# Pooling chunks of the even layer moved, in pieces, into its attention; half of its output projection too; four heads at once in its softmax steps

## The reference, cut to what matters

```
z = rms_norm(x) @ w_in               # 1280 columns: u 512 | q 512 | k 128 | v 128
# pooling: 4 groups of 128 channels, trailing windows 2, 4, 8, 16
diff_g = window_sum(u_g) / count - u_g
ya_g   = (diff_g @ w_pool_g) * scale
# attention: 8 query heads, 2 key heads, chunks of 64; a chunk reads itself and the 2 before it
p  = exp(s - m) / (sum exp(s - m) + exp(sink - m)),  m = max(max s, sink)
yb = p @ v
x  = x + concat(ya, yb) @ w_out
x  = x + ffn(rms_norm(x))
```

## Time and profile before

| | |
|---|---|
| median of 3 runs | 1284.98 us (1284.3 to 1286.83) |
| profiled execution | 1286.24 us, its span 1284.1 us |
| PE busy | 1229.3 us, 96% |
| DVE busy | 814.2 us, 63% |
| POOL busy | 700.0 us, 55% |
| ACT busy | 262.0 us, 20% |
| mean granted TensorE clock | 0.986 |

### The profile page before, as it was taken

The page is one execution under the profiler, slowest core; times in us unless marked ns, Lnnn a source line. Parts: engine busy times, 40 slices in busy tenths (PEclk is TensorE's granted clock), DMA queues, the critical chain, the costliest instruction groups (busy, mean ns, idle before and its releaser), DMA issues.

```text
span 1284.1 us, 24797 instructions
## 1 busy us (share of the span) xinstructions
PE 1229.3 (96%) x9677; PEld 1193.1 (93%) x9677; DVE 814.2 (63%) x1174; ACT 262.0 (20%) x514; POOL 700.0 (55%) x565
## 2 busy tenths in 40 slices
PE   6978999999999999999999998999999999999995
PEld 6966799999999999999999985799999999999995
DVE  6988477777777732116544688666877887872221
ACT  3015332111111110002111165422112112110002
POOL 6732257556656666665644432156665665566661
PEclk9989999999999999999999999899999999999998
DMA  6311123222223232233222310132222222323221
GB/s 211 116 58 34 36 67 99 82 92 87 82 84 95 82 99 87 94 98 110 83 84 65 102 60 23 34 109 89 93 82 86 93 82 82 95 84 96 88 79 71
DMA packets 35524, 108.91 MB, mean 85 GB/s; under 512 B 5984, under 2 KB 7792, under 8 KB 35472
## 3 DMA queue, kind: packets, MB, share of 16 engines
q1 hardware_dynamic: 29232, 102.51, 24.7%
q10 hardware_dynamic: 6240, 5.64, 1.5%
HBM read 103.00 MB, written 5.13 MB: 84 GB/s over the span
## 4 chain that ended last, share of the span: by engine, by line
PE 88%; DVE 8%; ACT 2%; issue 1%; DMA 0%; POOL 0%; ACTq 0%; POOLq 0%; SPq 0%; DVEq 0%
PE psum L423 28%; PE psum L425 27%; PE psum L424 27%; DVE even_winsum L1340 1%; PE psum L741 1%; PE psum L608 1%; DVE small L1561 1%; DVE even_rope_swapped L1322 1%; PE psum L756 1%; DVE even_diff L1343 0%; DVE gate_tmp L1490 0%; PE psum L582 0%; PE psum L556 0%; DVE diff_probs L1576 0%; DMA x<-in_x 0%
## 5 line engine op out<-in xcount | busy, mean ns | idle before, releaser
L423 PE MATMUL psum<-h_hi,w_hi 128*128 128x272 f32 x2032 | 593.5, 292 | 15.1 <-DVE h_lo L1177 10.8
L425 PE MATMUL psum<-h_hi,w_lo 128*128 128x272 f32 x2032 | 588.5, 290 | 0.0
L424 PE MATMUL psum<-h_lo,w_hi 128*128 128x272 f32 x2032 | 585.5, 288 | 0.0
L394 POOL TENSOR_TENSOR w_lo<-w_raw,w_hi 128x1024 fp32r<-128x1024 f32 x187 | 464.9, 2486 | 15.6
L423 PEld LDWEIGHTS psum<-h_hi,w_hi 128*128 128x128 f32 x2032 | 383.0, 188 | 20.3 <-issue 17.0
L424 PEld LDWEIGHTS psum<-h_lo,w_hi 128*128 128x128 f32 x2032 | 383.7, 189 | 0.2
L425 PEld LDWEIGHTS psum<-h_hi,w_lo 128*128 128x128 f32 x2032 | 382.9, 188 | 0.0
L391 POOL TENSOR_TENSOR tick<-tick 1x1 f32<-1x1 f32 x183 | 38.8, 212 | 530.0 <-PE psum L425 529.6
L423 PE MATMUL psum<-y_hi,w_hi 128*128 128x272 f32 x832 | 246.8, 297 | 3.6 <-DVE x L1193 2.8
L425 PE MATMUL psum<-y_hi,w_lo 128*128 128x272 f32 x832 | 242.9, 292 | 0.0
L424 PE MATMUL psum<-y_lo,w_hi 128*128 128x272 f32 x832 | 241.8, 291 | 0.0
(11 more groups left out here) (205 smaller groups left out, 1104.7 us busy)
## 6 DMA issues: line engine op xcount, KB each, us to landing
w_raw<-in_weights SPq DMA_DIRECT2D x187, 512.0 KB, 3.5
x<-in_x SPq DMA_DIRECT2D x8, 272.0 KB, 5.5
out_y<-x SPq DMA_DIRECT2D x8, 272.0 KB, 2.4
out_diff_v_new<-odd_dv ACTq DMA_DIRECT2D x1, 1024.0 KB, 6.2
out_diff_k_new<-odd_kT ACTq DMA_DIRECT2D x1, 1024.0 KB, 4.5
even_rope<-in_rope ACTq DMA_DIRECT2D x1, 544.0 KB, 3.5
odd_rope<-in_rope ACTq DMA_DIRECT2D x1, 544.0 KB, 4.0
consts<-in_consts ACTq DMA_DIRECT2D x1, 384.5 KB, 4.8
```

What stands on the lines that cost most here:

```text
L394: pool.tensor_tensor(w_lo[:, k], w_raw[:, k % RAW], w_hi[:, k].bitcast(F32), ALU.subtract).then_inc(w_ready, 1)
L423: pe.matmul(out, wh, xh[:, cols], start=first and n == 0, stop=False)
L424: pe.matmul(out, wh, xl[:, cols], start=False, stop=False)
L425: ins = pe.matmul(out, wl, xh[:, cols], start=False, stop=last and n == len(pairs) - 1)
```

## The change

The even input projection now has 6 chunks in the order v, k, q0 to q3 (`EVEN_PROJ`), in accumulators 2, 3, 1, 0, 3, 2. The four pooling chunks, in the order of the groups 3, 2, 1, 0, come as pieces of 1 to 8 input tiles between the steps of attention (`EVEN_U`: key (unit, place), place 0 is between values and scores, place 1 behind the scores), and a pooling product behind the values at units 2, 4, 6 and 7 (`EVEN_POOL`). They all use accumulator 3. The pooled half of the output projection starts at unit 7 (`EVEN_OUT`); its chunks 2 to 7 come behind the last values. DVE's window sums are cut up over units 0 to 6. ScalarE takes a product into `even_diff` and from there into `y_hi`, and DVE makes `y_lo` from these two. The softmax steps handle four heads in one instruction, with the negated sinks kept. ScalarE's order is now copy of unit u, then exponentials of u+2, for u = 1 on; five output DMAs of ScalarE stand behind the exponentials of unit 2. `probs`, `probsT` and the attention output no longer lie in the place of `h_hi` and `h_lo`, and `out_norm` makes the norm of all eight chunks at once. The diff, cut to its core (unchanged counters shifted by it are left out):

```diff
+EVEN_PROJ = 6
...
-        EVEN_FILL = {0: 0, 1: 1, 2: 2, 4: 3, 6: 4, 8: 5, 9: 6}
+        POOL_ORDER = [3, 2, 1, 0]
+        EVEN_U = {(-1, 1): (0, 0, 8), (0, 0): (1, 0, 1), (0, 1): (1, 1, 4), (1, 0): (1, 4, 5), (1, 1): (1, 5, 8),
+                  (2, 1): (2, 0, 4), (3, 0): (2, 4, 5), (3, 1): (2, 5, 8), (4, 1): (3, 0, 4), (5, 0): (3, 4, 5),
+                  (5, 1): (3, 5, 8)}
+        EVEN_POOL = {2: 0, 4: 1, 6: 2, 7: 3}
+        EVEN_OUT = {(7, 1): (0, 0, 3), (8, 0): (0, 3, 4), (9, 1): (1, 0, 4)}
...
-            return 1 if first and n == 2 else 2 + n % 2
+            return (2, 3, 1, 0, 3, 2)[n] if first else 2 + n % 2
...
-                    if n >= (2 if n_norm else 3):
+                    if n_norm and n >= 2:
                         pe.wait_ge(evac, ev0 + n - 1)
+                    if not n_norm and n == 3:
+                        pe.wait_ge(rms_ready, 1)
+                    if not n_norm and n >= 4:
+                        pe.wait_ge(evac, 2 if n == 4 else 1)
...
-                if u < 2:
+                if u == 0:
+                    pe.wait_ge(rope_done, 3)
+                    pe.wait_ge(evac, 4)
+                elif u == 1:
                     pe.wait_ge(rope_done, 5)
-                    pe.wait_ge(y_lo_done, 3)
+                    pe.wait_ge(v_out, 1)
...
+            def pool_fill(i, k0, k1):
+                s = EVEN_PROJ + i
+                if k0 == 0:
+                    pe.wait_ge(w_ready, s + 1)
+                    if i < 2:
+                        pe.wait_ge(evac, EVEN_PROJ + 1 if i else EVEN_PROJ - 1)
+                    else:
+                        pe.wait_ge(pool_out, i - 1)
+                ins = tiles(3, s, h_tiles(k0, k1), k0 == 0, k1 == KC)
+                if k1 == KC:
+                    ins.then_inc(slab_done, 1)
+            def pool_product(i):
+                if i == 0:
+                    pe.wait_ge(in_even, 16 * NEVEN)
+                if i < 3:
+                    pe.wait_ge(evac, EVEN_PROJ + i + 2)
                 else:
...
+                    pe.wait_ge(pool_out, 3)
+                pe.wait_ge(diff_ready, i + 1)
+                g = POOL_ORDER[i]
+                for half in range(2):
+                    ins = pe.matmul(psum[:, 6 + half, 0:HALF], e_wpool[:, g],
+                                    e_diff[:, g, half * HALF:(half + 1) * HALF], start=True, stop=True)
+                ins.then_inc(side_mm, 1)
+            def pooled_fill(m, i0, i1):
+                s = S_EVEN_OUT + m // 2
+                if i0 == 0:
+                    pe.wait_ge(w_ready, s + 1)
+                    if m == 0:
+                        pe.wait_ge(pool_out, 4)
+                    else:
+                        pe.wait_ge(x_upd, m)
+                for i in range(i0, i1):
+                    if m == 0:
+                        pe.wait_ge(pool_lo, i + 1)
+                    c = POOL_ORDER[i]
+                    ins = tiles(3, s, [(4 * (m % 2) + c, y_hi[:, c], y_lo[:, c])], i == 0, i == 3)
+                if i1 == 4:
+                    ins.then_inc(slab_done if m % 2 else mid_done, 1)
+            def even_fill(u, place):
+                if (u, place) in EVEN_U:
+                    pool_fill(*EVEN_U[u, place])
+                if place == 0 and u in EVEN_POOL:
+                    pool_product(EVEN_POOL[u])
+                if (u, place) in EVEN_OUT:
+                    pooled_fill(*EVEN_OUT[u, place])
...
             even_scores(0)
+            even_fill(-1, 1)
             even_scores(1)
-            pe.wait_ge(evac, EVEN_IN)
-            pool_product(0, 3)
             for u, (b, c) in enumerate(EU):
                 (q0, nq), _, runs = even_block(b)
-                pe.wait_ge(p_norm, 2 * u + 2)
+                pe.wait_ge(p_norm, u + 1)
                 pr = probs[u % 2][:, :].rearrange("p (h k) -> p h k", h=4)
                 for kb, (_, kn) in enumerate(runs):
                     for j in range(4):
                         ins = pe.transpose(psum[0:kn, 2 * (u % 2) + kb, j * nq:(j + 1) * nq],
                                            pr[0:nq, j, kb * P:kb * P + kn], ident[0:nq, 0:nq])
                 ins.then_inc(p_turned, 1)
-                if u in EVEN_FILL:
-                    out_fill(S_EVEN_OUT, EVEN_FILL[u], 0, EVEN_IN)
                 if u >= 1:
                     even_values(u - 1)
+                even_fill(u, 0)
                 if u + 2 < len(EU):
                     even_scores(u + 2)
+                even_fill(u, 1)
...
-            for m in range(len(EVEN_FILL), KC):
-                out_fill(S_EVEN_OUT, m, 0, EVEN_IN)
-            pe.wait_ge(y_lo_done, 9)
+            for m in range(2, KC):
+                pooled_fill(m, 0, 4)
+            pe.wait_ge(y_lo_done, 5)
             for m in range(KC):
                 pe.wait_ge(x_upd, KC + m - 1)
-                out_chunk(S_EVEN_OUT + 4 + m // 2, m, 2 + m % 2, h_hi, h_lo, 4)
+                out_chunk(S_EVEN_OUT + 4 + m // 2, m, 2 + m % 2, e_hi, e_lo, 0)
...
+            def pooled(i):
+                g = POOL_ORDER[i]
+                ac.wait_ge(side_mm, i + 1)
+                ac.activation(halves(e_diff[:, g]), pair(3), ACT.Copy,
+                              scale=const("pool_scale")[:, g:g + 1]).then_inc(pool_out, 1)
+                ac.wait_ge(pool_out, i + 1)
+                ac.activation(y_hi[:, g], e_diff[:, g], ACT.Copy).then_inc(pool_hi, 1)
...
-                for c in range(2):
-                    ac.wait_ge(negm, 2 * u + c + 1)
-                    for j in (2 * c, 2 * c + 1):
-                        o(ac.activation(probs[u % 2][0:nq, j * 256:j * 256 + nk], S[0:nq, j, 0:nk], ACT.Exp,
-                                        bias=sm[:, 4 + j:5 + j], scale=0.125, accum_out=sm[:, 8 + j:9 + j]))
-                    ac.activation(sm[:, 16 + 2 * c:18 + 2 * c], sm[:, 12 + 2 * c:14 + 2 * c], ACT.Exp)\
-                        .then_inc(e_ready, 1)
+                ac.wait_ge(negm, u + 1)
+                for j in range(4):
+                    o(ac.activation(probs[u % 2][0:nq, j * 256:j * 256 + nk], S[0:nq, j, 0:nk], ACT.Exp,
+                                    bias=sm[:, 4 + j:5 + j], scale=0.125, accum_out=sm[:, 8 + j:9 + j]))
+                ac.activation(sm[:, 16:20], sm[:, 12:16], ACT.Exp).then_inc(e_ready, 1)
...
             even_exp(0)
-            pooled(4, 0, 3)
+            even_turned(0)
             even_exp(1)
-            even_turned(0)
             for u, (b, c) in enumerate(EU):
-                if u + 1 < len(EU):
-                    even_turned(u + 1)
+                if u >= 1:
+                    even_turned(u)
+                if c == 0 and b >= 1:
+                    even_out(b - 1)
+                if u in EVEN_POOL:
+                    pooled(EVEN_POOL[u])
                 if u + 2 < len(EU):
                     even_exp(u + 2)
-                if c == 1:
-                    (q0, nq), _, _ = even_block(b)
-                    ac.wait_ge(o_ready, u + 1)
-                    ac.activation(h_hi[:, 4:8, q0:q0 + nq],
-                                  psum[:, 4 + b % 2, 0:4 * nq].rearrange("p (j q) -> p j q", j=4),
-                                  ACT.Copy).then_inc(y_hi_done, 1)
+                if u == 0:
+                    dma(io["swa_v_new"][0], e_v[:, 3], out_done)
+                    dma(io["swa_v_new"][1, 0:P - SMP], e_vc[SMP:P, :], out_done)
+                    dma(io["swa_v_new"][1, P - SMP:P], e_v[0:SMP, 4], out_done)
+                    ac.wait_ge(rope_done, 1)
+                    dma(io["swa_k_new"][:, 0], e_kT[:, SEQ - P:SEQ], out_done)
+                    dma(io["swa_k_new"][:, 1], e_kT[:, KEYS - P:KEYS], out_done)
+            even_out(4)
...
+            def pool_add(g, i):
+                w = 2 ** (i - 1)
+                src = e_u[:, g] if i == 1 else e_w[:, i % 2]
+                dst = e_w[:, (i + 1) % 2]
+                lo = 2 * w - 1
+                o.wait()
+                o(ve.tensor_tensor(dst[:, lo:UE], src[:, lo:UE], src[:, lo - w:UE - w], ALU.add))
+            def pool_diff(g):
+                u, w = e_u[:, g], POOL_W[g]
+                src = e_w[:, g % 2]
...
+            def pool_in(i):
+                ve.wait_ge(slab_done, EVEN_PROJ + i + 1)
+                o(grouped(e_u[:, POOL_ORDER[i]], 3, PS), evac)
+            def pooled_low(i):
+                g = POOL_ORDER[i]
+                ve.wait_ge(pool_hi, i + 1)
+                ve.tensor_tensor(y_lo[:, g], e_diff[:, g], y_hi[:, g].bitcast(F32), ALU.subtract).then_inc(pool_lo, 1)
...
+                sinks = neg_sinks[0:nq, :].rearrange("p (g c j) -> p g c j", g=2, c=2)[:, :, c]
+                ve.wait_ge(s_ready, 2 * u + 2)
+                o(ve.tensor_reduce(sm[:, 0:4], s_even(u)[0:nq, :, 0:nk], AX.X, ALU.max))
+                o.wait()
+                o(ve.scalar_tensor_tensor(sm[:, 4:8].rearrange("p (g j) -> p g j", g=2),
+                                          sm[:, 0:4].rearrange("p (g j) -> p g j", g=2), -0.125, sinks, ALU.mult, ALU.min))
```

(50 more changed lines are left out.)

182 lines of the change are left out of this document (56 added, 126 removed).

## The result

The changed kernel takes 1291.93 us (median of 6 runs, 1291.34 to 1292.95), the kernel before 1285.51 us in the runs beside it (median of 6, 1284.3 to 1286.83): ratio 1.005, interval 1.004 to 1.006. It is 6.4 us slower; 9.6 had been forecast. The profiled execution took 1292.20 us, its span 1290.1 us, against 1284.1 us before.

The account below looks back on a forecast made before the run. PE bounds the kernel (busy 96%), so only its waits and slow clock count. Work 81.7 + 1.5 + 4.7 + 13.0 + 2.2 + 4.5 + clock 6.3 = 113.9 against 104.3 us: 9.6 slower, 1294.5 us; range 1276 to 1303.

Parts of the forecast that it names:

- Nothing later on matters: Behind the first attention chunk of the output projection: no new PE waits, later norms cost nothing, stage's difference kept.
- In front of the loop, nothing lost: Before the attention loop: k and q ready in time, a 6.05 us pooling chunk hides unit 0's normalising; 0 us.
- ScalarE's queue and unit 1's transposes, 6.2 us: PE waits 1.5 us for unit 1's softmax, then 4.7 before scores(3) for a copy behind exponentials and five DMA issues.
- The three products, 13.0 us: Units 2, 4, 6: POOL's splits hold DVE's differences and the scaling behind them; PE waits 4.3, 4.7 and 4.0 us.
- POOL misses DVE: Rival, chance 0.20: differences escape POOL's pass at the products, whose waits fall to 0.8, 1.1 and 0.3; 1278.6 us.
- The end of the loop, 2.2: Waits of 0.8 us for unit 7's softmax, 1.1 for the last difference, 0.3 for the last lower half.
- Accumulator 3, 4.5: Pooled output chunks 2 to 7 each wait for the previous addition: 0.8 us five times, 0.5 for chunk 2.
- Softmax, 1 us less on DVE for each unit: Four heads at once drop six small instructions, some 1.05 us per unit, hidden unless PE waits for DVE.
- The clock, 6.3: Clock dips behind four waits of 4 us and more: 1.7 us at each product, 1.2 behind scores(3).
- clock never recovers: Rival, chance 0.15: recurring waits keep the clock at 0.57 from 72 to 120 us, costing 15 us; 1305 us.

Follow-up runs that it names:

- e3_no_splits: The changed kernel with POOL leaving out the splitting of weight slabs 9 to 13, nothing else moved: 1275.18 us (one run).
- e7: The changed kernel with windows a unit earlier, pooled halves in two accumulators, three second-pooling-chunk pieces behind scores(1), first scaling before first normalising: 1275.93 us.
- e8: The changed kernel with windows a unit earlier, pooled halves in two accumulators, and ScalarE's five output DMAs behind the loop: 1278.80 us (one run).
- e2: The changed kernel with each group's window sums and difference a unit earlier, in units 0, 2 and 4: 1281.28 us.
- e5: The changed kernel with the softmax steps in two halves of two heads again: 1298.84 us.
- e1: The changed kernel with pooled halves 2, 4 and 6 of the output projection in accumulator 1, the others in 3: 1285.83 us.
- e4: The kernel before with one part of the change alone, softmax steps for four heads in one instruction: 1293.22 us.
- e9: e7 with the softmax of the even units in halves of two heads again: 1283.75 us.
- e10_q3_first: e7 with DVE's rotation and copy of the fourth group of q ahead of the maximum of unit 0: 1275.08 us.

## Why the prediction was right, and where it was wrong

The direction, the place and the cause of the largest term were right: 112.85 us for the stage where 113.9 was forecast. How near the size came is in part luck, as terms that failed offset each other. Of the 3.2 us between the forecast difference (9.6) and the measured one (6.4), 1.1 lie in the stage and 1.7 in the clock of the odd attention. By its steps:

- **Nothing later on matters**: right for the waits, wrong in taking the stage's difference to the end. 1.7 us of it went in the clock of the odd attention. Of the 0.8 behind that, 0.6 are a single wait for issue that before's trace has and after's hasn't; why is open.
- **In front of the loop, nothing lost**: the step that failed most. Waits of 4.8 us and 3.0 of clock. I used POOL's hold-up for the windows and walked `rotate` and the normalising at free durations, though they too have two inputs in SBUF; e3_no_splits removed the two longer waits.
- **ScalarE's queue and unit 1's transposes, 6.2 us**: didn't come. The DMA issues overlap the exponentials, and PE, late and at half clock from the front, got to scores(3) only at 73.44 us, just as the copy was out (72.79 and 0.60). The 7.8 us of the front stand in the place of this term. The chain is real: 2.0 us in e3 and 2.85 in e7. The issues weren't its length (e8), and 0.92 us in the earlier trace rows is for two of them.
- **The three products, 13.0 us**: right in mechanism, shown by e2 and e3, and 8.4 in size. 3.7 and 3.9 stood for 4.3 and 4.7; the third was the rival "POOL misses DVE", for one product of three. I had priced that rival for all three or none, though its condition, 0.2 us between two starts, is open for each anew; e5 has the third product with both instructions held.
- **The end of the loop, 2.2**: 2.8 (1.1 for softmax, 1.7 for the last difference), near.
- **Accumulator 3, 4.5**: 5.1 in waits, and 1.13 us from half to half where 0.8 was taken, of which the wait's row holds 0.9. e1 took away 6.0 over these halves.
- **Softmax, 1 us less on DVE for each unit**: right (the maximum over four heads took 1.225 us, 1.23 was forecast), but "hidden, unless DVE is what PE waits for" was the whole point. e4 and e5 show that this edit alone is worth some 7 us with either sign, and the text had costed it at nothing.
- **The clock, 6.3**: 7.3. Dips stood behind the waits of 2.3, 3.7 and 3.9 us and none behind those of 0.9, 1.1 and 1.7. The third forecast dip was missing for want of its wait, and the front had one of its own.

The rule of the Trainium skill (TensorE: Matmul & The Clock Gate, "HAM oscillation — how this bites in real kernels"), that waits in every round throttle the array each time, stood beside the rival "clock never recovers". Here each wait of 2.3 us or more did have its dip, but the granted clock came back to 1.00 in between, as from 88 to 100 us above, and the rival's 1305 stayed out. The skill's rule on DVE and GpSimd (SBUF — State Buffer, "Who interferes with whom") is borne out by e3: 1387 ns against 176. On one point the trace differs: by the page whoever issues first keeps the other out, yet DVE's 32 columns start at 77.89, 0.10 us ahead of POOL, and take 1.18 us. The difference is small, and how exact the start of a row of POOL is no run shows.

Open: what the remainder of 2.5 us is. It stands in e3 as well, which has no clock loss: 95.2 = 81.7 + 11.0 of waits + 2.5. In the kernels with two accumulators it is 0.7 to 1.7, so about 1 us goes with the single accumulator and is outside the waits' rows; the rest may be my 2.1 us for the small units.

## What to carry to other kernels

When a weight split on GpSimd is triggered by PE's own progress, every DVE instruction that PE's next step waits for has a place relative to it: put two-input and small instructions ahead of the trigger, and let only the one that is waited for stand behind. Walk every DVE instruction near a split at its held duration, the ones that didn't move too. Whether to batch small steps had a different sign by the order here: it lost in the order of before, where PE waited for the softmax chain, and gained in the two later ones (e5, e9), where every small instruction stood in DVE's queue near a split and more of them met it. The size couldn't be told ahead in any of the three tries (e4, e5, e9), so measure it again after each reordering.

## What the runs showed of the hardware

- A DVE instruction of 2 to 32 columns that meets a split took 1.0 to 2.3 us in the rows above instead of 0.15 to 0.2, even when its row starts up to 0.1 us before POOL's (77.89 against 77.99; 93.85 against 93.91, here a TENSOR_SCALAR with one input tile). One that started 0.15 us before it got through (116.66 against 116.81).
- DMA issues in ScalarE's queue run beside its own ACTIVATEs (one starts at 71.58, within 71.33 to 71.81), at 0.36 to 0.45 us each.
- The clock's dips in the same odd attention fall differently from kernel to kernel: losses of 1.5, 3.1 and 4.8 us go with 686.1, 687.4 and 689.0 us for the same instructions. Executions of one kernel, e1_two_accs, take 1284.41 to 1289.22 us, with a mean granted clock of 0.990 down to 0.984.
- Best version: e10_q3_first, 1275.08 us, ratio 0.9918 (0.9902 to 0.9935) to before; e7_front_fill can't be told from it.
